# Attention in a two-block transformer on one core: a ring of three score places, and one conditioning part summed on GpSimd

## The reference

```
# conditioning, in each of three layers: six vectors of 1024, for latent and for context tokens
sh_a, sc_a, g_a, sh_f, sc_f, g_f = split(silu(c) @ w_ada + b_ada, 6)
# layer 0, heads "A": 4 heads, each the difference of two softmaxes over 768 keys
a  = softmax(s1) - lam * softmax(s2);   oa = a @ v
# layer 0, heads "B": 8 heads of plain softmax attention over 768 keys (latent queries)
ob = softmax(q @ k.T * scale) @ v
new = x + g_a * (concat(rmsnorm(oa), ob) @ w_out)
out = new + g_f * swiglu(modulate(rmsnorm(new), sh_f, sc_f))
# layer 1: 8 global heads (768 keys; context queries see 256), 8 neighbourhood heads (scores + bias)
# layer 2: 16 heads, window of 128 to each side, context keys, and a sink column in the softmax
y = p @ v for each;  x = layer_norm(alpha * x + g * (y @ w_out));  then a gated FFN with a short convolution
```

## Time and profile before

| | us |
|---|---|
| median of 3 runs | 2819.86 |
| lowest, highest | 2813.25, 2821.51 |
| profiled execution, its own time | 2824.43 |
| its span | 2822.6 |
| PE busy in the span | 2500.3 (89%) |
| DVE busy | 1611.4 (57%) |
| ACT busy | 940.0 (33%) |
| POOL busy | 375.0 (13%) |

### The profile page before, as it was taken

How to read it: one execution, slowest core, us unless ns; L and a number is a source line. 1 busy time by engine, 2 the same in 40 slices (tenths; PEclk the granted TensorE clock), 3 DMA queues, 4 the chain that set the end, 5 groups by cost and what they waited for, 6 DMA issues and landing times.

```text
span 2822.6 us, 32852 instructions
## 1 busy us (share of the span) xinstructions
PE 2500.3 (89%) x13098; PEld 1948.4 (69%) x13098; DVE 1611.4 (57%) x2674; ACT 940.0 (33%) x1722; POOL 375.0 (13%) x355
## 2 busy tenths in 40 slices
PE   5797899899999899887978999999968778999995
PEld 5685574678877776554447888888856553878774
DVE  4448572565665633877357655554565873645355
ACT  2325451321212322555132322332332561423232
POOL 0010001111021100000101122122221001000122
PEclk9899999899999999999989999999978999999998
DMA  6132301643433220200113223331211202322221
GB/s 227 47 104 78 106 1 46 231 165 134 165 127 127 90 73 29 92 27 14 60 52 127 85 90 113 116 120 60 75 47 59 90 1 75 110 100 90 82 82 45
DMA packets 78743, 251.27 MB, mean 89 GB/s; under 512 B 6400, under 2 KB 11264, under 8 KB 70144
## 3 DMA queue, kind: packets, MB, share of 16 engines
q1 hardware_dynamic: 69696, 220.22, 22.9%
q0 software_dynamic: 7600, 24.75, 2.3%
q10 hardware_dynamic: 1296, 4.21, 0.4%
HBM read 239.72 MB, written 9.44 MB: 88 GB/s over the span
## 4 chain that ended last, share of the span: by engine, by line
PE 69%; DVE 13%; ACT 5%; issue 4%; POOL 2%; DMA 0%; POOLq 0%; DVEq 0%; ACTq 0%
PE PS L844 9%; PE PS L845 9%; PE PS L846 9%; PE PS L822 7%; PE PS L879 5%; PE PS L880 4%; PE PS L881 4%; PE PS L706 4%; DVE SM L1454 3%; PE PS L654 3%; PE PS L651 3%; PE PS L652 3%; ACT HT L2011 3%; PE PS L719 2%; PE PS L752 2%
## 5 line engine op out<-in xcount | busy, mean ns | idle before, releaser
L844 PE MATMUL PS<-HH,WH 128*128 128x512 f32 x1056 | 418.4, 396 | 6.0 <-DVE WL L1621 4.4
L845 PE MATMUL PS<-HL,WH 128*128 128x512 f32 x1056 | 416.4, 394 | 0.0
L846 PE MATMUL PS<-HH,WL 128*128 128x512 f32 x1056 | 415.8, 394 | 0.0
L1852 ACT ACTIVATE WH<-STG 128x1024 fp32r<-128x1024 f32 (+1 forms) x204 | 198.9, 1023 | 330.2 <-PE PS L881 245.1
L879 PE MATMUL PS<-WH,AH 128*128 128x512 f32 x616 | 252.0, 409 | 47.3 <-DVE AL L1718 31.6
L1253 DVE SCALAR_TENSOR_TENSOR ACC<-ADAW,CS,ACC 128x1024 f32<-128x1024 f32 x208 | 268.4, 1329 | 27.9 <-DMA ACC<-in_b_ada 19.1
L1621 DVE TENSOR_TENSOR WL<-STG,WH 128x1024 fp32r<-128x1024 f32 (+1 forms) x204 | 239.9, 1217 | 67.9 <-ACT WH L1852 67.3
L880 PE MATMUL PS<-WL,AH 128*128 128x512 f32 x616 | 248.3, 403 | 0.0
L881 PE MATMUL PS<-WH,AL 128*128 128x512 f32 x616 | 248.0, 403 | 0.0
L844 PEld LDWEIGHTS PS<-HH,WH 128*128 128x128 f32 x1056 | 202.0, 191 | 48.7 <-issue 5.0
L651 PE MATMUL PS<-PW,HTH 128*128 128x512 f32 (+3 forms) x528 | 202.6, 384 | 35.5 <-DVE PW L1313 14.4
(11 more groups left out here) (177 smaller groups left out, 3968.1 us busy)
## 6 DMA issues: line engine op xcount, KB each, us to landing
ADAW<-in_w_ada SPq DMA_DIRECT2D x136, 512.0 KB, 4.0
STG<-in_w_up SPq DMA_DIRECT2D x66, 1024.0 KB, 6.7
STG<-in_w_down SPq DMA_DIRECT2D x20, 1024.0 KB, 5.1
STG<-in_w_ffn_out SPq DMA_DIRECT2D x10, 1024.0 KB, 7.3
STG<-in_ev_w_in SPq DMA_DIRECT2D x8, 1024.0 KB, 5.8
spill<-X POOLq DMA_DIRECT2D x14, 512.0 KB, 6.4
STG<-in_w_in SPq DMA_DIRECT2D x6, 1024.0 KB, 8.5
REG<-spill POOLq DMA_DIRECT2D x10, 512.0 KB, 8.4
```

Source lines behind the costliest of these rows:

```text
L844: e.matmul(PS[:, b, 0:T], h_, HH[gi][:, c, :], start=first, stop=False)
L845: e.matmul(PS[:, b, 0:T], h_, HL[gi][:, c, :], start=False, stop=False)
L846: return e.matmul(PS[:, b, 0:T], l_, HH[gi][:, c, :], start=False, stop=last)
```

## The change

In A and in layers 1 and 2, score n goes to place n % 3, where place 0 is banks 0 and 1, place 1 banks 2 and 3, place 2 banks 4 and 5; turned pieces take banks 6 and 7. The result of item q goes to columns 384 to 511 of the second bank of place 2q % 3, behind the 256 score columns that the bank holds. A pair of scores waits for the exponentials of the scores that were in its two places, and for a result behind them. ACT copies a result between the two exponentials of a pair. In A the turns come an item later and the result matmuls of item i-3 come straight after the scores of item i. B keeps its places.

Of the conditioning, parts 1, 10 and 16 are summed on GpSimd by new code (`ada_here`): one product and one addition of 128x1024 for each block and vector, with the blocks loaded from GpSimd's queue. Parts 2 and 3 are loaded from GpSimd's queue too and added by DVE in B, one or two a pair. Nothing of the conditioning is left in layer 0's projection, in A on DVE, or in DVE's part of the attention of layers 1 and 2, but for the end of parts 10 and 16 (the ones-matmuls and copies), at item 40 of 48 and 26 of 32.

```diff
+    def ring_bank(self, n):
+        return 2 * (n % 3)
+    def scores(self, name, n):
+        b = 2 * (n % 2) if name == "B" else self.ring_bank(n)
+        return self.PS[:, b:b + 2, :].rearrange("p b n -> p (b n)")
+    def result(self, name, q):
+        return self.ps(("out", name, q))[:, 0:P] if name == "B" else self.PS[:, self.ring_bank(2 * q) + 1, 384:512]
...
+ADA_POOL, ADA_LOAD = (1, 10, 16), (1, 2, 3, 10, 16)
+ADA_PAIR = {1: 40, 2: 26}
...
-    bg = ada(1, 4)
-    project(0, bg)
-    step(bg, 16)
+    project(0)
...
+    class PairAtt:
+        def score_pair(self, p, mms):
+            for n in (2 * p, 2 * p + 1):
+                self.free(k.ring_bank(n))
+                self.free(k.ring_bank(n) + 1)
...
+            for n in (2 * p, 2 * p + 1):
+                for b in range(2):
+                    freed[k.ring_bank(n) + b] = [k.ac_exp((self.name, n))]
...
+        def out_one(self, i, v):
+            b, pt = k.ring_bank(2 * i) + 1, self.turned_p(i)
+            self.free(b)
+            self.copied(i, 6)
+            for c in range(6):
+                m = e.matmul(k.result(self.name, i), pt[:, c * P:(c + 1) * P], v(c), start=c == 0, stop=c == 5)
+            m.then_inc(*k.pe_out.up((self.name, i)))
+            freed[b] = [k.ac_out((self.name, i))]
...
@@ heads A on PE
         a.score_pair(i, [full_mm(QT[64 * s:64 * s + 64, h, (tt - 2) * P:(tt - 1) * P], KT[64 * s:64 * s + 64, h, :])
                          for s in range(2)])
-        if i:
-            a.turn(i - 1, 2 * (i - 1) % 6, 6, k.dv_p(("A", i - 1)))
+        if i >= 3:
+            a.out_one(i - 3, lambda c, h=(i - 3) // 4: V[:, c, h * P:(h + 1) * P])
         if i >= 2:
-            a.out_one(i - 2, 6, lambda c, h=(i - 2) // 4: V[:, c, h * P:(h + 1) * P])
-        step(bg)
+            a.turn(i - 2, 2 * (i - 2) % 6, 6, k.dv_p(("A", i - 2)))
...
@@ heads B, on each engine
-                steps(bg, p)
+                step(bg, 1 + (p % 3 == 0))
...
@@ heads A on DVE
-    for i in range(17):
-        if i:
-            mix(i - 1)
-            total_inverse("A", 2 * (i - 1))
+    for i in range(18):
         if i < 16:
             w.wait_ge(*k.pe_score(("A", i)))
             for n in (2 * i, 2 * i + 1):
                 largest("A", n, 768)
-        if i:
-            a_tail(i - 1)
-        if i < 16:
-            step(bg)
+        if 1 <= i <= 16:
+            mix(i - 1)
+            total_inverse("A", 2 * (i - 1))
+        if i >= 2:
+            a_tail(i - 2)
...
@@ layers 1 and 2 on ACT
                 for n in (2 * p, 2 * p + 1):
                     place_free(n)
                     power(name, L, n, it["nk"], n % n_p)
+                    if p >= 2 and n % 2 == 0:
+                        result(p - 2)
...
@@ new on GpSimd
+    def ada_here(i):
+        blocks = row_blocks(i, i + 1)
+        step(blocks)
+        step(ada(i, i + 1))
+        w.wait_ge(*k.ac_cs())
+        for c in range(8):
+            step(blocks)
+            w.wait_ge(*k.row_block_in[c % 2]((i, c)))
+            for v in vecs(i):
+                a, col = k.ACC[:, v * 1024:(v + 1) * 1024], (16 if ADA[i][0] else 0) + v * 8 + c
+                raw = k.ADAW[:, c % 2 * 1024:(c % 2 + 1) * 1024]
+                y = k.LOW[:, 0:1024] if v < vecs(i)[-1] else raw
...
+                e.tensor_scalar(y, raw, k.CS[:, col:col + 1], None, ALU.mult).then_inc(*k.pl_prod.up((i, c, v)))
+                w.wait_ge(*(k.pl_ada((i, c - 1, v)) if c else k.bias_in[v](i)))
+                w.wait_ge(*k.pl_prod((i, c, v)))
+                e.tensor_tensor(a, a, y, ALU.add).then_inc(*k.pl_ada.up((i, c, v)))
...
+    bg, blocks = ada(2, 4), row_blocks(2, 4)
+    step(bg)
+    step(blocks, 10)
+    step(bg, 10)
+    step(blocks, 10)
```

More of the change, by code:

```diff
@@ L538, in sync_program @@
                 neighbourhood(hp)
+        if L == 1:
+            for s in range(2):
+                ada_free[s] = [k.ada_added(10, 6 + s, 1)]
         ffn(L, ada(11, 16) if L == 1 else iter(()))
@@ L557, in ada @@
             layer, j, _ = ADA[i]
-            for _ in range(9):
+            for _ in range(0 if i in ADA_POOL else 9):
                 yield
@@ L1019, in tensor_program @@
                               "v": [lambda i, h=h, VB=VB: VB[:, i, h * 64:(h + 1) * 64] for h in hs]})
-    pairs(a, items, bg, lambda bg, p: step(bg, 2))
+    pairs(a, items, bg)
     step(bg, 100)
@@ L1245, in ada @@
             layer, j, _ = ADA[i]
-            for c in range(8):
+            for c in range(0 if i in ADA_POOL else 8):
                 for v in vecs(i):
@@ L1255, in ada @@
                 yield
-            yield
+            if i not in ADA_POOL:
+                yield
             for v in vecs(i):
@@ L1531, in packed_pairs @@
                     normal(L, L, n, it["nk"], 4)
-            if it is not None:
-                steps(bg, p)
+            if p == at:
+                step(bg, 2)
     def layer_norm(stage, L, tt, ready):
@@ L1823, in vector_program @@
         turned_up(n)
-    pairs("B", 0, bg, lambda bg, p: step(bg, 2))
+    bg = ada(1, 4)
+    pairs("B", 0, bg)
     step(bg, 100)
@@ L2008, in power, with pairs @@
     def power(name, L, n, nk, at):
-        S = PS[:, 2 * (n % 2):2 * (n % 2) + 2, :].rearrange("p b n -> p (b n)")
         w.wait_ge(*k.dv_max((name, n)))
-        e.activation(k.att[L]["HT"][:, at * 768:at * 768 + nk], S[:, 0:nk], ACT.Exp, bias=k.small("att", n),
+        e.activation(k.att[L]["HT"][:, at * 768:at * 768 + nk], k.scores(name, n)[:, 0:nk], ACT.Exp, bias=k.small("att", n),
                      accum_out=k.small("att", n, 1)).then_inc(*k.ac_exp.up((name, n)))
-    def pairs(name, L, bg, steps):
+    def pairs(name, L, bg, at=None):
         items = items_of(k, L)
@@ L2202, in scalar_program @@
             power("A", 0, n, 768, n % 6)
+            if i >= 3 and n % 2 == 0:
+                a_result(i - 3)
         if i >= 2:
-            a_result(i - 2)
-        step(bg)
-    a_head(15)
-    a_result(14)
-    a_result(15)
+            a_head(i - 2)
+    a_result(13)
+    for i in (14, 15):
+        a_head(i)
+        a_result(i)
     e.drain().then_inc(*k.ac_end.up("A"))
@@ L2438, in gpsimd_program @@
     step(bg, 100)
-    bg = ada(1, 4)
-    project(0, bg)
-    for i in range(16):
-        step(bg)
+    project(0)
+    for c in (6, 7):
+        w.wait_ge(*k.ada_added(0, c, 1))
+    ada_here(1)
     KR = k.latents()[2]
```

244 lines of the change are left out of this document (127 added, 117 removed).

## The result

The changed kernel takes 2826.17 us (median of 10 runs, 2824.38 to 2831.13) against 2818.33 for the kernel before beside it (2812.75 to 2822.08): a ratio of 1.0031, 95% interval [1.0021, 1.0041]. It is slower by a little, and my forecast leaned the other way. Its profiled execution took 2828.28 us with a span of 2826.4, 3.8 more than the span of before; so the profiles show half of the 7.8 us between the medians.

A forecast was written before the change was run, and what follows sets the result against it. PE, busy 2500.3 of 2822.6 us, was the bound, so only stages where it waits could give much. Terms -14, +20, +12, -11.5 and -11 summed to -4.5: 2815 us against the runs' median 2819.86, range 2788 to 2840.

The forecast's parts named there:

- layer 1's term: Layer 1's attention: additions leave DVE and the ring helps, but GpSimd holds normalisations; -11.5 us, bounds -5 to -26.
- layer 2's term: Layer 2's attention: first items gain 0, then the ring gives -2 for each four items; -11 us, bounds -5 to -20.
- Projection: Layer 0's projection: PE's 13.28 us pause nearly vanishes without ADAW's loads ahead of the weights; -14 us, bounds -8 to -15.
- Heads A: Heads A: result matmuls wait for their own item's exponential, 6.6 us an item; +20 us, bounds +12 to +37.
- A's wait is hidden: Rival in A: the exponential comes early, about 4.1 us an item; A gains 11, kernel 2784 us; chance 0.13.
- the pauses pull the clock down for good: Rival in A: every stretch behind a pause runs at clock 0.50; A +37, kernel 2832 or 2840 us; chance 0.17.
- my upper bound: Heads A's upper bound: all work at half the clock, 8.7 us an item, +37 us.
- Heads B: Heads B: DVE's additions +1, ones-matmuls +4, late first block +6, clock drop +1; +12 us, bounds +5 to +20.
- About 61 us, or two groups: Layer 1: length of GpSimd's sum, 16 products taken at 1.5 us and 16 additions at 2.34.
- The half with bias: Layer 1's four groups with bias: 28.1 us each against 30.40, -9.2 in all, and the moved finish +6.
- GpSimd doesn't hold DVE: Rival: layer 1 gains 12 more and layer 2 some 8 more, kernel 2795 us; chance 0.18.
- The ring does nothing: Rival in layers 1 and 2: DVE is the limit; layer 1 -5, layer 2 -3, kernel 2829 us; chance 0.12.

The follow-up runs named there:

- the run with narrow additions: The changed kernel with DVE's 16 additions of parts 2 and 3 in B cut to 8 of 1024 columns: 2822.50 us.
- the run without sums: The changed kernel with GpSimd's products and additions of parts 10 and 16 cut to 8 of 1024 columns: 2797.16 us.
- the ring alone: The changed kernel with parts 10 and 16 loaded from SP's queue and summed by DVE at their old steps, ring kept: 2815.35 us.
- the four edits' kernel: The changed kernel with A's results in place (2q+2) % 3, part 2's first blocks loaded ahead, part 10 on DVE, part 16 on DVE in the last FFN: 2773.44 us.

## Why the prediction was wrong

**The direction was wrong; most mechanisms were found.** I forecast -4.5 us by the profile; the five stages gave +10.9. The projection gained 2.7 us more than I had put, and A, B, layer 1 and layer 2 came out worse by 4.7, 2.4, 6.1 and 4.9. Two steps failed: the length of GpSimd's product in layer 1's term, and the finish of part 16 (its ones-matmuls and copies), which layer 2's term had at nothing without a reason.

*Projection.* -14 forecast, -16.7 measured. The pause went: PE's wait of 13.28 us for the second piece is 0.2 in the changed kernel. That needed the additions on DVE gone as well as their loads: with the order of the queue alone turned, a wait of 6.2 us stays. What the term left out is the clock. Before, PE worked for 127.55 us in this stage at 0.94, and in the changed kernel for 124.42 at 1.00:

```profile
71.00:213.50 142.50, 127.55 (x618) 108.59 (x618) 61.40 (x123) 42.49 (x94) 13.80 (x14) 0.94 0.22 74
```

*Heads A.* +20 forecast, +24.7 measured. The wait is there with the length worked out (2.14 us against about 2.1). The start took 14.5 us for 13, the twelve periods 83.7 for 79.2, and the tail 14.5 for 15. The pairs of items have the mean that I forecast, 6.7 for 6.6; the period of 9.1 at the start and a pair of 7.2 and 7.9 later on make up the rest. The rival "A's wait is hidden" fell, and the one that the pauses pull the clock down for good too, since the low clock came in every second item. That rival, and my upper bound, were also summed wrongly: 13 + 12 x 8.7 + 15 less 88 is +44 and not +37, which makes the rival 2839 and, with B at its upper bound, 2847.

*Heads B.* +12 forecast, +14.4 measured. The stall at the first block was named, in its place; it lasted 5.40 us and the item 11.40 against 6.72 for the item of before that holds a part's finish. But the sum came near by luck: DVE's added time, which I had at +1, is worth 6.2 by the run with narrow additions, and the first block, the matmuls and the clock, which I had at +11 together, are the other 8.2.

*Layer 1.* This is the step that failed most in size: -11.5 forecast, -5.4 measured. "About 61 us, or two groups" rested on a product of 1.5 us, taken between bounds of 1.0 and 2.34; it takes 2.96, outside the bounds, and the sum some 85 us. The third group, which I had freed, still took 29.1 us where the run without sums takes 24.2: 4.9. So the third and fourth group gained 2.6 us (54.4 against 57.0) and not 8. The first two, which I had at 0, gained 3.2 (57.2 against 60.4), by luck as far as my sum goes; the ring alone takes 59.0 for them. Before, these four groups were:

```profile
1110.50:1140.30 29.80, 22.51 (x148) 13.01 (x148) 24.49 (x46) 15.16 (x38) 2.02 (x4) 0.83 0.28 86
1140.30:1170.90 30.60, 26.06 (x210) 17.30 (x210) 28.39 (x53) 16.25 (x43) 0.00 (x0) 0.89 0.55 192
1170.90:1203.10 32.20, 29.52 (x218) 18.55 (x218) 22.80 (x48) 17.19 (x45) 0.00 (x0) 0.89 0.01 2
1203.10:1227.90 24.80, 22.57 (x209) 15.21 (x208) 19.23 (x44) 15.84 (x43) 0.00 (x0) 1.00 0.08 26
```

The half with bias was to gain 3.2 with the finish in it, and it took 131.3 us against 130.9. For a bias group I had 28.1 us, and it took 28.9: four times 0.8. The layer's last item took 13.8 us instead of 12.3, at a granted clock of 0.88 instead of 1.00. The finish at item 40 cost 6 us as priced. (The 0.154 us that I set beside the 0.77 of the earlier trace rows is the median of a line with mixed shapes; its undisturbed 128x8 operations took 0.17, which changes nothing.)

*Layer 2.* -11 forecast, -6.1 measured. The ring's gain was right (18.5 to 16.3 for four items), and so were the first ten items, which gained nothing (56.3 us in both kernels). What I left out of this term is the finish of part 16: before, it fell into an item of 6.83 us beside ones of 5.0 to 5.5, in a stretch that DVE bounds (25.63 us busy of 27.60, PE 21.03); at item 26 PE is busy for some 14.8 of 16.3 us, and that item takes 9.38 us instead of 5.05:

```profile
2304.51:2307.96 3.45, 3.45 (x6) 1.04 (x6) 0.27 (x1) 0.60 (x1) 0.00 (x0) 0.56 0.00 0
```

The ones-matmuls alone last 3.45 us there, at a granted clock of 0.56; the same four took 1.9 us in the last FFN of the four edits' kernel. The runs bear the price out: with GpSimd's operations cut but the finish in place, layer 2's attention took 143.3 us, and with neither 138.8.

I had moved the finish in layer 1's term and not in layer 2's. With it my sum would have been near 0, and with the 4.9 us of the product's real time near +5.

The rival "GpSimd doesn't hold DVE" fell with the run without its sums. "The ring does nothing" fell too: alone it gives 20 us in the two layers. The range, 2788 to 2840, held the time, but it was so wide that it held both directions; the sum inside it had the wrong one.

## What to carry to other kernels

When a ring of buffers is shared by things of different age, work out the place of each at every step: the same formula 2q % 3 is the free place for results two items behind and the busy one for three, and it cost 38 us of 2820. Work moved to GpSimd beside a busy VectorE isn't free of VectorE: price it by how long GpSimd's instructions are, since each could hold a DVE normalisation here until it ended (1.85 us for one of 0.35), and compare that with what DVE would have needed itself. And a step that is moved takes its last part with it: ask what the engine that does it has to spare at the new place.

## What the runs showed of the hardware

GpSimd's product of 128x1024 fp32 with a column of scalars (2.96 us) is slower than its addition of two such tiles (2.40), though it reads one large input less; I had expected the opposite. A pause of 1.34 us and one of 0.46 in each item of 5.77 left the clock at 1.00 for 35 us, with pauses of 2.14 us the matmuls behind the pause ran at 1.00 in one item and at 0.57 in the next. And the DVE operations that read PSUM were not lengthened beside GpSimd: in layer 1 the maximum of 768 columns took 0.95 us with it and 0.96 without, the copy of 256 columns 0.41 and 0.42.
